# The six key and query products of the scan's later rounds on VectorE instead of GpSimd

## The reference

```python
def ssd_gla_layer(x, ...):
    u = rms_norm_2(x, norm_w) @ w_in                      # 1024 -> 5408 columns
    z_a, xbc, dt_raw, q_b, k_b, v_b, gate_lr, g_b = split_cols(u, EVEN_SPLITS)
    ...                                                   # SSD scan: decay weights times C.B, times xs, 16 heads
    y_a = rms_norm_2(ssd_chunked_scan(xs, dt, a, bm, cm, d) * silu(z_a), ssd_norm_w)
    log_decay = log_sigmoid(gate_lr @ gate_w2 + gate_b) / 16
    o_b = gla_chunked(q_b, k_b, v_b, log_decay)           # 8 heads of 64 keys, 128 values, chunks of 64 tokens
    o_b = rms_norm_2(o_b, gla_norm_w) * silu(g_b)
    return x + concatenate([y_a, o_b]) @ w_out

def gla_chunked(q, k, v, log_decay):
    gcs = cumsum(log_decay) within a chunk;  ref = its value in the chunk's middle
    scores = einsum(q * exp(gcs - ref), k * exp(ref - gcs))            # products qe and ka of the kernel
    chunk_kv = einsum(k * exp(g_last - gcs), v)                        # product kb
    o_inter = einsum(q * exp(gcs), prev_states)                        # product qg
    return causal(scores) @ v + o_inter
```

## Time and profile before

| | |
|---|---|
| median of 3 runs | 837.35 us |
| the profiled execution | 836.93 us, its span 835.2 us, 1.73 us around it |
| TensorE busy | 825.7 us, 99% of the span |
| VectorE, ScalarE, GpSimd busy | 618.9, 504.9, 127.2 us (74%, 60%, 15%) |
| the four rounds of the scan | about 513 to 643 us of the span |
| granted TensorE clock | 0.998 of full speed over the span |

### The profile page before, as it was taken

The page is one execution under the profiler, slowest core; times in us unless marked ns, Lnnn a source line. Parts: engine busy times, 40 slices in busy tenths (PEclk is TensorE's granted clock), DMA queues, the critical chain, the costliest instruction groups (busy, mean ns, idle before and its releaser), DMA issues.

```text
span 835.2 us, 16954 instructions
## 1 busy us (share of the span) xinstructions
PE 825.7 (99%) x6832; PEld 799.4 (96%) x6832; DVE 618.9 (74%) x1029; ACT 504.9 (60%) x875; POOL 127.2 (15%) x120
## 2 busy tenths in 40 slices
PE   9999999999999999999999999999999999999997
PEld 8999999999999999999999999999998999888896
DVE  6657888887666689777664478999898696568765
ACT  7446566555444576555554368787967654356755
POOL 1000000000000305443441100043515010000002
PEclk9999999999999999999999999999999999999999
DMA  9744334345655536655565525646545375554431
GB/s 320 264 160 142 139 112 167 127 149 179 181 192 183 174 101 201 205 180 181 197 191 191 188 93 164 198 140 196 171 140 177 111 232 186 180 176 128 127 101 51
DMA packets 39853, 139.81 MB, mean 167 GB/s; under 512 B 4432, under 2 KB 5088, under 8 KB 39648
## 3 DMA queue, kind: packets, MB, share of 16 engines
q1 hardware_dynamic: 38160, 135.90, 50.8%
q10 hardware_dynamic: 1616, 2.84, 1.0%
HBM read 137.65 MB, written 1.06 MB: 166 GB/s over the span
## 4 chain that ended last, share of the span: by engine, by line
PE 90%; DVE 5%; ACT 2%; POOL 1%; issue 1%; DVEq 0%; ACTq 0%; POOLq 0%
PE ps L1839 67%; PE ps L1904 5%; PE ps L1863 4%; PE ps L1842 4%; DVE weights_lo L1100 2%; PE ps L2024 1%; PE ps L2050 1%; PE ps L2312 1%; PE ps L1960 1%; PE ps L2330 1%; PE ps L1866 1%; PE ps L2320 1%; PE ps L2035 1%; ACT weights_hi L557 1%; PE ps L1953 1%
## 5 line engine op out<-in xcount | busy, mean ns | idle before, releaser
L1100 DVE TENSOR_TENSOR weights_lo<-raw_weights,weights_hi 128x1024 fp32r<-128x1024 f32 x251 | 313.5, 1253 | 84.0 <-ACT weights_hi L557 82.7
L557 ACT ACTIVATE weights_hi<-raw_weights 128x1024 fp32r<-128x1024 f32 x250 | 262.1, 1053 | 133.5 <-PE ps L1839 55.0
L1839 PE MATMUL ps<-x_hi,weights_hi 128*128 128x256 f32 (+3 forms) x1184 | 341.6, 289 | 0.2
L1839 PE MATMUL ps<-x_lo,weights_hi 128*128 128x256 f32 (+3 forms) x1184 | 333.7, 282 | 0.0
L1839 PE MATMUL ps<-x_hi,weights_lo 128*128 128x256 f32 (+3 forms) x1184 | 333.1, 281 | 0.0
L1839 PEld LDWEIGHTS ps<-x_hi,weights_hi 128*128 128x128 f32 x1184 | 222.8, 188 | 6.6 <-issue 5.1
L1839 PEld LDWEIGHTS ps<-x_lo,weights_hi 128*128 128x128 f32 x1184 | 222.9, 188 | 0.7 <-issue 0.5
L1839 PEld LDWEIGHTS ps<-x_hi,weights_lo 128*128 128x128 f32 x1184 | 223.2, 189 | 0.0
L1839 PE MATMUL ps<-y_lo,weights_hi 128*128 128x256 f32 (+1 forms) x488 | 137.4, 282 | 0.0
L1839 PE MATMUL ps<-y_hi,weights_hi 128*128 128x256 f32 (+1 forms) x488 | 137.2, 281 | 0.0
L1839 PE MATMUL ps<-y_hi,weights_lo 128*128 128x256 f32 (+1 forms) x488 | 137.1, 281 | 0.0
(11 more groups left out here) (288 smaller groups left out, 1183.5 us busy)
## 6 DMA issues: line engine op xcount, KB each, us to landing
raw_weights<-weights_in SPq DMA_DIRECT2D x251, 512.0 KB, 3.8
arena<-decay_rows ACTq DMA_DIRECT2D x8, 256.0 KB, 3.8
masks<-masks_in SPq DMA_DIRECT2D x1, 1186.0 KB, 7.7
raw_weights<-weights_in SPq DMA_DIRECT2D x4, 256.0 KB, 4.6
hidden<-xT_in SPq DMA_DIRECT2D x3, 272.0 KB, 5.0
hidden<-xT_in SPq DMA_DIRECT2D x1, 276.0 KB, 3.1
gate_w<-gate_w_in ACTq DMA_DIRECT2D x1, 256.0 KB, 3.7
out<-arena ACTq DMA_DIRECT2D x1, 256.0 KB, 2.1
```

The lines of the kernel that those rows point to most:

```text
L557: a.sig(A(whi[:, s * CW:(s + 1) * CW], raw[:, (c % RAW) * CW:(c % RAW + 1) * CW], ACT.Copy), "hi_ready")
L1100: d.sig(TT(wlo[:, s * CW:(s + 1) * CW], raw[:, (c % RAW) * CW:(c % RAW + 1) * CW], whi[:, s * CW:(s + 1) * CW].bitcast(F32), ALU.subtract) ...
L1839: ins = mm(bank(BANK_OF[no])[:, 0:b - a], wt, x_[:, kt, a:b], start=s0, stop=s1)
```

## The change

The six products of rounds 1 to 3 move from GpSimd's list to VectorE's. GpSimd keeps the decay weights and the sum of squares. VectorE makes the product of `kb` first (`key_product`): in round 1 after `ssd_args(3)` and ahead of `gla_norm(0)`, in rounds 2 and 3 after `feed(("ek", p))` and ahead of `ssd_y(2p)`. The other five (`products`) come after `gla_norm(0)` in round 1 and after `ssd_args(2p+1)` in rounds 2 and 3, ahead of `z_half(("eg", 2p))`. TensorE's scores wait for the round's own `ka`.

```diff
@@ gpsimd
-            def gla_keys(p):
-                k = p % 2
-                pool.wait_ge(S("gla_exp"), p + 1)
-                pool.wait_ge(S("out_taken"), K_TAKEN[p])
-                need(pool, "gla_o", p - 1)
-                g.settle()
-                g.sig(nc.gpsimd.tensor_tensor(kb[:, k, :], kb[:, k, :], e_k[:, k, :], ALU.mult), "gla_kl")
-
-            def gla_products(p):
-                k = p % 2
-                g.settle()
-                g.step(nc.gpsimd.tensor_tensor(ka[:, k, :], ka[:, k, :], e_k[:, k, :], ALU.mult))
-                for e in range(2):
-                    rows = slice(64 * e, 64 * e + 64)
-                    g.settle()
-                    g.step(nc.gpsimd.tensor_tensor(qg[rows, k, e, :], eg[rows, k, :], e_q[rows, k, :], ALU.mult))
-                    g.settle()
-                    ins = nc.gpsimd.tensor_tensor(qe[rows, k, e, :], em[rows], e_q[rows, k, :], ALU.mult)
-                    g.sig(ins, "gla_qk") if e else g.step(ins)
-
-            g.n.update(gla_qk=1, gla_kl=1, m_ready=4)
+            g.n.update(m_ready=4)
             for p in range(1, 4):
                 ssd_weights(2 * p)
-                gla_keys(p)
-                gla_products(p)
@@ vector
-            def first_products():
-                dve.wait_ge(S("gla_exp"), 1)
-                d.sig(TT(kb[:, 0, :], kb[:, 0, :], e_k[:, 0, :], ALU.mult), "gla_kl")
-                d.sig(TT(ka[:, 0, :], ka[:, 0, :], e_k[:, 0, :], ALU.mult), "gla_ka")
+            def key_product(p):
+                k = p % 2
+                dve.wait_ge(S("gla_exp"), p + 1)
+                d.settle()
+                d.sig(TT(kb[:, k, :], kb[:, k, :], e_k[:, k, :], ALU.mult), "gla_kl")
+
+            def products(p):
+                k = p % 2
+                need(dve, "gla_o", p - 1)
+                d.sig(TT(ka[:, k, :], ka[:, k, :], e_k[:, k, :], ALU.mult), "gla_ka")
                 for e in range(2):
                     rows = slice(64 * e, 64 * e + 64)
-                    d.step(TT(qg[rows, 0, e, :], eg[rows, 0, :], e_q[rows, 0, :], ALU.mult))
-                    ins = TT(qe[rows, 0, e, :], em[rows], e_q[rows, 0, :], ALU.mult)
+                    d.step(TT(qg[rows, k, e, :], eg[rows, k, :], e_q[rows, k, :], ALU.mult))
+                    ins = TT(qe[rows, k, e, :], em[rows], e_q[rows, k, :], ALU.mult)
                     d.sig(ins, "gla_qk") if e else d.step(ins)
...
-            first_products()
+            key_product(0)
+            products(0)
...
                     ssd_args(3)
+                    key_product(1)
                     gla_norm(0)
+                    products(1)
                     feed(("ez", 2))
...
                     feed(("ek", p))
+                    key_product(p)
                     ssd_y(u)
...
                     ssd_args(u + 1)
+                    products(p)
                     if p == 2:
                         gla_low(0)
@@ tensor
-                pe.wait_ge(S("gla_ka"), 1)
+                pe.wait_ge(S("gla_ka"), p + 1)
```

More of the change, by code:

```diff
@@ L399, in build @@
         CONVS = [t for t in HALF if t[0] in ("eb", "ec", "ex")]
-        K_TAKEN = [taken[FIRST_OUT["ek", p]][1] for p in range(4)]
         STORES = ((0, 0, 2), (0, 2, 5), (0, 5, KT), (1, 0, 4), (1, 4, KT))
```

## The result

| | before | after |
|---|---|---|
| median | 837.38 us (6 runs) | 841.96 us (6 runs, 841.14 to 842.82) |
| ratio of the times | | 1.0049, 95% interval 1.0038 to 1.0059 |
| the profiled execution | 836.93 us | 842.16 us, its span 840.2 us |

The account below looks back on a forecast made before the run. TensorE, busy for 99% of the span, was taken to bound the kernel, so only its waits change the time. Later arrivals of +1.7 us (round 2) and +1.3 (round 3) made +3.0, forecast 840.3 us, range 836.6 to 842.2.

Parts of the forecast that it names:

- Round 1: VectorE's split for the chunk TensorE wants at 570.29 comes 1.3 us later, ending at 570.9; TensorE waits 0.6.
- a loss of a whole GpSimd instruction: VectorE beside GpSimd on the SBUF port: each hold-up 1.1 us by the page's rule, the sum below 1.5 us more.
- its own price of 0.8: Loss taken for a VectorE instruction that meets a GpSimd decay weight (128x384): 0.8 us, bounds 0 and 1.1.
- Round 2: VectorE's split starts at 606.1 and ends 1.7 us later, so TensorE's wait for ssd_y at 615.87 ends 1.7 later.
- Round 3: VectorE's five products delay the split for the third eo1 tile, whose first matmul moves 1.3 us, to 645.6.
- TensorE's gain at `ssd_heads(7)`: Round 3: GpSimd's last decay weights come in time; 1.0 us saved, 0.1 perhaps lost at ssd_args(7), net -0.9.
- the tile: Third eo1 tile in round 3: its first matmul, the fifth of L1904, moves from 644.28 to 645.6, +1.3 us.
- The sum: Whole kernel: +1.7 (round 2) + 1.3 (round 3) = +3.0 us, forecast 840.3 us, chance 0.51.
- Nothing later gives it back: Behind the scan TensorE runs on its own with only short waits, so the +3.0 us stays to the end.
- The wash: Rival: GpSimd's hold-ups cost VectorE as much as the products; only round 3's +1.3 is left, 838.6 us; chance 0.27.
- the faster case: Rival: ssd_y 0.82 earlier, ssd_heads(7) loses its 1.0, third eo1 tile on time; -1.8, 835.5 us; chance 0.12.
- The third rival: Each hold-up is a whole GpSimd instruction: +0.9 in round 1, +0.6 in round 2, 841.8 us; chance 0.10.

Follow-up runs that it names:

- e2: Kernel before with only round 3's six products on VectorE, those of rounds 1 and 2 on GpSimd: 839.54 us, ratio 1.0023.
- e8: Kernel before with only round 3's six products on VectorE, placed behind gla_norm(2): 838.53 us against 837.71, ratio 1.0012.
- f4: Kernel before with GpSimd's round 3 reordered, decay weights of ssd_heads(7) ahead of the four query products: 838.64 us, ratio 1.0013.
- e3: Changed kernel with five extra matmuls, result unread, ahead of the three eo1 tiles: median 842.09 us, in two groups.
- f3: Changed kernel with extra unread matmuls in both long TensorE waits, four before ssd_y(5)'s wait, five before the eo1 tiles: 841.49 us, ratio 1.0047.
- e5: Changed kernel with VectorE's products of rounds 1 to 3 only 4 columns wide: 836.87 us against 837.71, ratio 0.9993.
- f2: Kernel before with only round 2's six products on VectorE, those of rounds 1 and 3 on GpSimd: 838.75 us, ratio 1.0012.
- e1: Changed kernel with round 3's six products back on GpSimd, rounds 1 and 2 on VectorE: 839.76 us against 837.69, ratio 1.0021.
- e4: Changed kernel with round 3's five products moved up behind gla_norm(2): 841.63 us, ratio 1.0043, in two groups.

## Why the prediction was right, and where its size was off

**Round 1: right.** The split for the chunk wanted at 570.29 was forecast to end at 570.9. In the changed kernel VectorE shows

```profile
565.64 0.42 DVE L1530 TENSOR_TENSOR arena<-arena 128x256 f32<-128x256 f32 x1
565.98 1.23 DVE L1533 TENSOR_TENSOR arena<-arena 64x256 f32<-64x256 f32 x1
567.14 1.23 DVE L1534 TENSOR_TENSOR arena<-arena 64x256 f32<-64x256 f32 x1
568.40 0.86 DVE L1533 TENSOR_TENSOR arena<-arena 64x256 f32<-64x256 f32 x1
569.18 0.42 DVE L1534 TENSOR_TENSOR arena<-arena 64x256 f32<-64x256 f32 x1
569.63 1.23 DVE L1077 TENSOR_TENSOR weights_lo<-raw_weights,weights_hi 128x1024 fp32r<-128x1024 f32 x1
```

Three products are held up, by 0.8, 0.8 and 0.45 us, and the split ends at 570.86. GpSimd's decay weights and its sum of squares, after:

```profile
565.73 2.37 POOL L484 TENSOR_TENSOR arena<-arena 128x384 f32<-128x384 f32 x2 [13.08 <-ACT arena L841]
568.24 0.74 POOL L490 TENSOR_TENSOR rinv_post<-rinv_post,arena 128x256 f32<-128x256 f32 x1
...
603.23 2.22 POOL L484 TENSOR_TENSOR arena<-arena 128x384 f32<-128x384 f32 x2 [15.55 <-ACT arena L841]
```

The second and third held product end at 568.37 and 569.26, each 0.27 to 0.28 us after the GpSimd instruction that runs when they start (568.10 and 568.98); so does the first (567.21, after the decay weight that ends at 566.93). The splits do the same: in the profiles of all kernels here 65 of them start during a decay weight of the scan, and each ends 1.08 to 1.09 us after it, whether it takes 1.4 or 2.0 us itself. So VectorE waits until GpSimd's instruction is over, and what it loses is what is left of that one when it starts, 0.96 us twice and 0.58 here, less 0.14. The Trainium skill's page "SBUF — State Buffer", section "Who interferes with whom", says that the one which starts first keeps the shared port for its whole instruction while the other waits; these rows agree. The prediction took from it a loss of a whole GpSimd instruction, 1.1 us, which the page doesn't say; its own price of 0.8, from rows, fits instructions that meet a decay weight near its start.

**Round 2: right in kind, 0.3 short.** `ssd_y(5)` came 2.02 late and not 1.7. One product and the operation behind it were held up, by 0.8 and 0.7 us, as forecast (two, 0.8 each):

```profile
603.33 1.24 DVE L1534 TENSOR_TENSOR arena<-arena 64x256 f32<-64x256 f32 x1
604.61 1.39 DVE L1503 TENSOR_TENSOR y_lo<-arena,y_hi 128x512 fp32r<-128x512 f32 x1
...
606.45 1.21 DVE L1077 TENSOR_TENSOR weights_lo<-raw_weights,weights_hi 128x1024 fp32r<-128x1024 f32 x1
```

The split started at 606.45, forecast 606.1. Counted from 560.5 as above, `ssd_y(5)` is 2.2 late, so the forecast is 0.3 to 0.5 short. Much of this is within what profiled executions differ by themselves: e2, e8 and f4, whose rounds 1 and 2 are those of before, stand 0.3 to 0.4 later at `ssd_y(5)` than the profile of before, counted in the same way.

**Round 3: right, 0.1 short, with one wait unforeseen.** TensorE's gain at `ssd_heads(7)` was 0.83 (forecast 0.9), the tile +1.4 on top of `ssd_y(5)` (forecast +1.3; e2 has 1.4 as well). The products there met nothing, 0.41 to 0.42 us each, 2.2 us in all. Unforeseen was the first wait, 1.11 us for `z_half(("ez", 7))`, which gives back the bank of the first `eo1` tile: it lies inside the same lateness, so by the sum it costs nothing of its own, but TensorE was idle twice in a row.

**The sum: one term missing.** "Nothing later gives it back" held; that nothing later adds to it did not. The sum's terms measured +2.0 and +1.4, so 3.4 for the forecast 3.0. The prediction counted a wait of TensorE at its own length alone and had no term for the granted clock behind it: 1.65 in the profiled execution, 1.55 in e3's, absent in e2's. That the rest of the medians' 4.6, about 1.2, is this term is the likely reading and not shown: with both waits filled, f3's median is only 0.5 lower.

**The rivals.** The wash and the faster case both rested on GpSimd's hold-ups being worth as much as the products: e5 puts what is won without them at 0.8 us, if at all. The third rival's time, 841.8, is the one that came, by another mechanism: no hold-up was the whole of a GpSimd instruction. That the median lies in the range, 0.2 below its end at 842.2, is therefore in part luck: the end was set for that rival, and the clock's term was in no part of it.

## What to carry to other kernels

An engine that is busy 74% on the mean can still pace a stage: of the 6.6 us that the eighteen products take alone (2.2 a round), 3.4 arrived at TensorE, net of what VectorE and TensorE got back, and 22.7 us taken from GpSimd were worth under one, if anything. Before work is put into an idle place, look at what the other engines do in just that stretch and who waits for the next result: here GpSimd made its decay weights in that stretch, or ScalarE stood behind it. A new wait of 1 to 2 us on TensorE is to be priced with the clock that can fall behind it, as a second term that comes in some executions.

## What the runs showed of the hardware that was not expected

The granted clock fell to 0.50 after TensorE had been idle for two waits of 1.11 and 0.73 us, and in e3 and f2 behind one of 1.8 us; behind the same waits it stayed at 1.00 in e2 (1.1 and 0.7 us) and in e1 (1.8 us). In the fourteen profiled executions it fell four times between the first eight microseconds and the last five: behind two of six waits of 1.8 us for `ssd_y(5)` and two of three pairs at the `eo1` tiles, and nowhere else. What decided in each case is not shown.

Each fall costs 1.54 to 1.65 us where it happens, and where TensorE waits again soon after, part of it comes back: f2's fall at 619 left +2.9 us, and the end of f2's span is +1.7 against before, since TensorE came later to `ssd_heads(7)` and no longer waited there for GpSimd. So such a kernel can have two times some 1.6 us apart, as e3 and e4 had, and a median over a few runs then depends on how many fell on each side; e1's runs show that it need not.

A held VectorE instruction ends a fixed time after the GpSimd instruction that holds it, whatever its own length is by then: 0.28 us after it for a product of 64x256 (25 of them beside decay weights in all profiles), 1.08 for a split (65 of them). So what it costs is read from the end of GpSimd's instruction and not from a loss per meeting.
